# Seven quarter products for eighteen feed-forward up chunks, and the first modulation beside the cross attention

## The reference

```
def _conv_ffn(h, w_up, conv_w, conv_b, w_down):
    up = h @ w_up                       # 256x1024 @ 1024x5632
    up = conv over time, width 3, one filter a column, + conv_b
    gate, val = up[..., :D_FF], up[..., D_FF:]      # D_FF = 2816
    return (jax.nn.silu(gate) * val) @ w_down       # 2816x1024
```

## Time and profile before

| | |
|---|---|
| median of three runs | 1548.22 us |
| the profiled execution | 1547.08 us, its span 1545.3 us |
| granted TensorE clock, mean | 0.999 |
| TensorE matmul busy | 1498.7 us (97%) |
| TensorE weight load busy | 837.4 us (54%) |
| VectorE busy | 465.5 us (30%) |
| ScalarE busy | 320.1 us (21%) |
| DMA | 513.52 MB, mean 332 GB/s |
| chain that ended last | TensorE 80%, DMA 15%, VectorE 2%, ScalarE 1% |

### The profile page before, as it was taken

One profiled execution on the slowest core, in us unless ns is written; L12 is line 12 of the kernel. 1 busy time (PEld: TensorE's weight loads), 2 busy tenths in 40 slices (PEclk: granted clock), 3 DMA queues, 4 the chain that ended last, 5 costly groups with the idle time before them and its releaser, 6 DMA issues.

```text
span 1545.3 us, 18172 instructions
## 1 busy us (share of the span) xinstructions
PE 1498.7 (97%) x7042; PEld 837.4 (54%) x7042; DVE 465.5 (30%) x894; ACT 320.1 (21%) x660; POOL 22.3 (1%) x43
## 2 busy tenths in 40 slices
PE   9999999999999999899999899999989999999997
PEld 8667888888888755444333243433324433433432
DVE  3664125665642243522111121211211212121212
ACT  2443142111113353211011011101101101110112
POOL 0000000000000000000000000000000000000000
PEclk9999999999999999999999999999999999999999
DMA  9635444777751355899999999999999999999996
GB/s 379 282 111 197 156 166 165 272 268 267 270 202 55 109 217 194 347 405 428 428 428 428 428 425 422 428 430 428 428 428 427 411 426 429 426 427 427 428 427 273
DMA packets 46720, 513.52 MB, mean 332 GB/s; under 512 B 5264, under 2 KB 5408, under 8 KB 8384
## 3 DMA queue, kind: packets, MB, share of 16 engines
q1 hardware_dynamic: 41984, 482.53, 76.0%
q0 software_dynamic: 4672, 30.06, 5.2%
HBM read 511.51 MB, written 1.06 MB: 332 GB/s over the span
## 4 chain that ended last, share of the span: by engine, by line
PE 80%; DMA 15%; DVE 2%; ACT 1%; issue 1%; SPq 0%; DVEq 0%; ACTq 0%
PE bank L1369 31%; PE bank L745 13%; DMA ring<-in_gate_w 13%; PE bank L1005 9%; PE bank L1014 5%; PE bank L1333 3%; PE bank L1493 3%; PE bank L1401 3%; PE bank L1220 2%; PE bank L856 2%; DMA ring<-in_down_w 2%; PE bank L1386 2%; PE bank L1173 1%; PE bank L1162 1%; PE bank L1113 1%
## 5 line engine op out<-in xcount | busy, mean ns | idle before, releaser
L1369 PE MATMUL bank<-ring,probs_slab 128*64 128x512 f32 x2824 | 630.5, 596 | 25.5 <-DMA ring<-in_gate_w 14.5
L1369 PEld LDWEIGHTS bank<-ring,probs_slab 128*64 128x64 f32 x2824 | 194.8, 137 | 412.9 <-issue 373.9
L2588 DVE TENSOR_TENSOR squares<-bank,tab 128x512 f32<-128x512 f32 x31 | 21.4, 692 | 463.9 <-PE bank L1386 463.8
L1005 PE MATMUL bank<-normed,ring 128*128 128x256 f32 x672 | 146.9, 379 | 0.0
L1005 PEld LDWEIGHTS bank<-normed,ring 128*128 128x128 f32 x672 | 127.6, 190 | 18.0 <-issue 0.8
L745 PE MATMUL bank<-normed,ring 128*128 128x256 f32 x384 | 84.5, 381 | 0.4 <-ACT normed L1658 0.4
L745 PEld LDWEIGHTS bank<-normed,ring 128*128 128x128 f32 x384 | 72.2, 190 | 11.7 <-ACT normed L1658 1.2
L1014 PE MATMUL bank<-big_slab,ring 128*128 128x256 f32 x352 | 77.6, 379 | 0.0
L2596 DVE TENSOR_TENSOR squares<-bank,tab 128x512 f32<-128x512 f32 x31 | 21.4, 692 | 180.6 <-PE bank L1386 180.6
L1014 PEld LDWEIGHTS bank<-big_slab,ring 128*128 128x128 f32 x352 | 66.9, 190 | 9.1
L1979 ACT ACTIVATE squares<-bank 128x512 f32<-128x512 f32 x31 | 18.5, 597 | 227.2 <-PE bank L1369 227.2
(11 more groups left out here) (396 smaller groups left out, 1274.2 us busy)
## 6 DMA issues: line engine op xcount, KB each, us to landing
ring<-in_down_w SPq DMA_DIRECT2D x61, 2048.0 KB, 17.3
ring<-in_up_w SPq DMA_DIRECT2D x60, 2048.0 KB, 19.0
ring<-in_gate_w SPq DMA_DIRECT2D x58, 2048.0 KB, 18.9
ring<-in_front_w SPq DMA_DIRECT2D x72, 1024.0 KB, 5.0
held_slab<-in_mod_w POOLq DMA_DIRECT2D x6, 1024.0 KB, 8.6
memory_slab<-in_mod_w POOLq DMA_DIRECT2D x6, 1024.0 KB, 8.2
cross_keys_slab<-in_mod_w POOLq DMA_DIRECT2D x6, 1024.0 KB, 7.1
probs_turned_slab<-in_mod_w POOLq DMA_DIRECT2D x6, 1024.0 KB, 7.6
```

Source lines behind the costliest of these rows:

```text
L1005: mm = pe.matmul(bank[bank_at][:, half * T:(half + 1) * T], w[:, (half * DC + k) * P:(half * DC + k + 1) * P], H[:, k, :], start=(k == 0), ...
L1369: mm = pe.matmul(to[half * SLOTS:(half + 1) * SLOTS, :], tokens(k), weights[:, half * D + i * HALF:half * D + (i + 1) * HALF], start=(k == ...
```

## The change

For the 18 chunks 4 to 21 the up product is made of seven quarter products, Winograd's form of Strassen's scheme. The weights of a chunk are seen as two by two blocks (half of the input features; gate or value columns), the input `H` as two by two blocks (half of the features; half of the tokens). Each quarter product has four matmuls of 128x128 weights against 128 tokens. VectorE makes sums of the input blocks once (`ff_input_sums`), and for each chunk four differences of weight blocks of 512 columns, two iterations ahead (`ff_weight_sums`; one of them written in place in the ring). A chunk has two banks now, `own` and `shared`. ScalarE copies the first product and then three shared ones out between the matmuls (`read_first`, `read_shared`, `read_own`), TensorE goes on in the same columns of the banks, and VectorE puts the quarters together (`ff_merge`) in `ff_u`, from which base and taps read. A bank pair is free for chunk `f` when chunk `f - 2` is merged.

On ScalarE and VectorE the base and taps of a seven-product chunk come one iteration later, and ScalarE's silu of a chunk stands ahead of the copies of the chunk two behind it (for odd chunks behind the copy of the first product).

Round 0 of the modulation moves ahead: three chunks behind the first three output products `wo`, one behind the statistics of the input, one behind the first head sums, one behind the first query scale, two behind the last cross normalisation. Its sums and transposes on TensorE stand before up 0 and before the second pair. Rounds 1 and 2 go to the iterations in `MODULATED_AT`. POOL loads the weights by the new order, the DFT tables after the last up product, and the router's weights behind `co3`.

```
+SEVEN = list(range(4, FF_CHUNKS))
+MODULATED_AT = {1: [8], 2: [9], 3: [10], 7: [11, 12], 9: [13], 11: [14, 15], 13: [16, 17], 15: [18, 19], 17: [20, 21],
+                19: [22], 22: [23]}
...
@@ gpsimd
             full(pool, "vx11")
             load_mod(0)
             load_mod(1)
-            pool.wait_ge(s_cross_scored, XHEADS)
-            load_mod(2)
+            for n in range(2, DC):
+                pool.wait_ge(s_mod, mod_steps(n - 1))
+                load_mod(n)
             full(pool, "co3")
-            load_mod(3)
...
+            for n in range(DC, MOD_ROUNDS * DC):
+                pool.wait_ge(s_mod, mod_steps(max(n - 2, DC)))
+                load_mod(n)
+            pool.wait_ge(s_ff_up, FF_CHUNKS)
             pool.dma_start(DFT[:, 0:5, :], dft_in[:, 0:5, :]).then_inc(s_in["dft"], 16)
...
@@ tensor
+            def ff_bank_free(f):
+                if f - 2 in SEVEN:
+                    pe.wait_ge(s_ff_sums, MERGES[f - 2] + 4)
+                    pe.wait_ge(s_ff_read, 3 * SEVEN.index(f - 2) + 3)
+                else:
+                    pe.wait_ge(s_ff_conv, f - 1)
+
+            def ff_seven(f, w):
+                i = SEVEN.index(f)
+                own, shared = bank[2 * (f % 2)], bank[2 * (f % 2) + 1]
+                t1, t2, t4 = ff_b[i % 2]
+                s1, s2, s3, s4 = ff_a
+
+                def product(to, b, a, start=False):
+                    for k in range(4):
+                        mm = pe.matmul(to, b[:, k * P:(k + 1) * P], a[:, k, :], start=(start and k == 0), stop=True,
+                                       skip_group_check=True)
+                    return mm
+
+                product(own[:, 0:P], weight_part(w, 0, 0), token_half(0, 0), start=True).then_inc(s_ff_seven, 1)
+                pe.wait_ge(s_ff_sums, WEIGHT_SUMS[f] + 4)
+                product(shared[:, 0:P], t2, s2, start=True)
+                product(shared[:, P:2 * P], weight_part(w, 0, 1), s3)
+                product(shared[:, 2 * P:3 * P], t1, s1).then_inc(s_ff_seven, 1)
+                pe.wait_ge(s_ff_read, 3 * i + 1)
+                product(own[:, 0:P], weight_part(w, 1, 0), token_half(1, 0))
+                pe.wait_ge(s_ff_read, 3 * i + 2)
+                product(shared[:, 2 * P:3 * P], weight_part(w, 1, 1), s4)
+                product(shared[:, P:2 * P], t4, token_half(1, 1)).then_inc(s_ff_up, 1)
...
+            sum_modulation(0, bank[5]).then_inc(s_mod_sum, 1)
...
+            turn_modulation(0, bank[6]).then_inc(s_mod_turned, 1)
             ff_pair(1, first=True, early=True)
-            for s in range(2, 6):
-                ff_pair(s)
-            ff_pair(6, between=first_modulation)
-            pe.wait_ge(s_mod_taken, 1)
-            for s in range(7, 11):
+            for s in range(2, 11):
                 ff_pair(s)
...
@@ scalar (read_first copies own 128 columns, read_shared 384 shared ones, read_own 128 to ff_u)
+            for f in range(1, FF_CHUNKS):
+                if f % 2 and f in SEVEN:
+                    read_first(f)
+                if f - 2 in SEVEN:
+                    ff_silu(f - 2, (f - 2) % 4)
+                if f % 2 == 0 and f in SEVEN:
+                    read_first(f)
+                if f in SEVEN:
+                    read_shared(f)
+                if f - 1 in SEVEN:
+                    ff_base(f - 1, (f - 1) % 4, f - 1, f < 5)
...
+                if f in SEVEN:
+                    read_own(f)
...
@@ vector
-            add_products(["wo0", "wo1", "wo2", "wo3"], "xn")
+            dve.wait_ge(s_silu_c, 1)
+            add_products(["wo0", "wo1", "wo2", "wo3"], "xn", lambda j: modulate(0, j) if j < 3 else None)
...
+            def ff_weight_sums(f):
+                i = SEVEN.index(f)
+                w, slot, here = ff_ring(f)
+                t1, t2, t4 = ff_b[i % 2]
+                dve.wait_ge(chunk_here[slot], here)
+                if i >= 2:
+                    dve.wait_ge(s_ff_up, SEVEN[i - 2] + 1)
+                b00, b10, b01, b11 = [weight_part(w, k_half, half) for half in range(2) for k_half in range(2)]
+                dve.tensor_tensor(t1, b01, b00, SUB).then_inc(s_ff_sums, 1)
+                dve.wait_ge(s_ff_sums, WEIGHT_SUMS[f] + 1)
+                dve.tensor_tensor(b01, b11, b01, SUB).then_inc(s_ff_sums, 1)
+                dve.tensor_tensor(t2, b11, t1, SUB).then_inc(s_ff_sums, 1)
+                dve.wait_ge(s_ff_sums, WEIGHT_SUMS[f] + 3)
+                dve.tensor_tensor(t4, b10, t2, SUB).then_inc(s_ff_sums, 1)
+
+            def ff_merge(f):
+                i = SEVEN.index(f)
+                one, six, seventh, fifth = [ff_read[i % 2][:, j * P:(j + 1) * P] for j in range(4)]
+                dve.wait_ge(s_ff_read, 3 * i + 2)
+                dve.tensor_tensor(six, six, one, ADD).then_inc(s_ff_sums, 1)
...
+                dve.tensor_tensor(seventh, seventh, six, ADD).then_inc(s_ff_sums, 1)
...
+                dve.tensor_tensor(ff_u[i % 2][:, 3 * P:4 * P], fifth, seventh, ADD).then_inc(s_ff_sums, 1)
+                dve.wait_ge(s_ff_up, f + 1)
+                dve.tensor_tensor(ff_u[i % 2][:, P:3 * P].rearrange("p (c n) -> p c n", c=2),
+                                  bank[2 * (f % 2) + 1][:, P:3 * P].rearrange("p (c n) -> p c n", c=2),
+                                  over(six, 2), ADD).then_inc(s_ff_sums, 1)
...
             for f in range(1, FF_CHUNKS):
+                if f == FF_CHUNKS - 1:
+                    ff_merge(f)
+                    ff_taps(f - 1, (f - 1) % 4)
+                    ff_taps(f, f % 4)
+                else:
+                    if f - 1 in SEVEN:
+                        ff_taps(f - 1, (f - 1) % 4)
+                    if f in SEVEN:
+                        ff_merge(f)
+                    else:
+                        ff_taps(f, f % 4)
                 if f > 4:
                     dve.wait_ge(s_ff_down, (f - 1) // 2 - 1)
                 ff_gate(f - 1, (f - 1) % 4)
...
+                if f + 2 in SEVEN:
+                    ff_weight_sums(f + 2)
...
+                for n in MODULATED_AT.get(f, ()):
+                    modulate(n // DC, n % DC)
```

More of the change, by code:

```diff
@@ L115 @@
 FF_AFTER = len(STREAM)
+SEVEN = list(range(4, FF_CHUNKS))
+WEIGHT_SUMS, MERGES, _n = {}, {}, 4
+for _f in range(1, FF_CHUNKS):
+    if _f in SEVEN:
+        MERGES[_f] = _n
+        _n += 4
+    if _f + 2 in SEVEN:
+        WEIGHT_SUMS[_f + 2] = _n
+        _n += 4
+MODULATED_AT = {1: [8], 2: [9], 3: [10], 7: [11, 12], 9: [13], 11: [14, 15], 13: [16, 17], 15: [18, 19], 17: [20, 21],
+                19: [22], 22: [23]}
 STREAM += (
@@ L481, in build_program, with token_half, weight_part, ff_ring @@
         ff_act = [BIG[:, 8 + i, :] for i in range(4)]
+        wide = lambda s, i: s[:, i:i + 2, :].rearrange("p a n -> p (a n)")
+        ff_b = [[wide(HOLD, 0), wide(HOLD, 2), wide(HOLD, 4)], [wide(HOLD, 6), wide(SQ, 0), wide(SQ, 2)]]
+        ff_a = [wide(VX, 2 * i).rearrange("p (k t) -> p k t", k=4) for i in range(4)]
+        ff_u = [wide(SQ, 4), wide(SQ, 6)]
+        ff_read = [wide(BIG, 14), ff_second_read]
+        def token_half(k_half, t):
+            return H[:, 4 * k_half:4 * k_half + 4, t * P:(t + 1) * P]
+        def weight_part(w, k_half, half):
+            at = (half * DC + 4 * k_half) * P
+            return w[:, at:at + 4 * P]
+        def ff_ring(f):
+            q = f if f < 2 else 2 + 3 * (f // 2 - 1) + f % 2
+            c = FF_FIRST + q
+            return ring[:, (c % RING + FRONT_SLOT) % RING, :], c % RING, 16 * (c // RING + 1)
+        def ff_source(f, half):
+            if f == 0:
+                return first_up[:, half, :]
+            if f in SEVEN:
+                return ff_u[SEVEN.index(f) % 2][:, half * T:(half + 1) * T]
+            return bank[f % 4][:, half * T:(half + 1) * T]
         block = stack.enter_context(nc.Block())
@@ L1041, in _, with ff_pair @@
             ff_up_matmuls(1, ff_up(1, slot, here, True), lambda k: normed_chunk(pe, "f", k))
-            def ff_pair(s, first=False, early=False, between=None):
+            def ff_pair(s, first=False, early=False):
                 k = s
@@ L1048, in ff_pair @@
                     slot, here = ff_chunk(2 + 3 * (k - 1) + i)
-                    if between:
-                        between(i)
-                    ff_up_matmuls((2 * k + i) % 4, ff_up(2 * s + i, slot, here, early))
+                    f = 2 * s + i
+                    w = ff_up(f, slot, here, early)
+                    if f in SEVEN:
+                        ff_seven(f, w)
+                    else:
+                        ff_up_matmuls(f % 4, w)
                 slot, here = ff_chunk(2 + 3 * (k - 1) + 2)
@@ L2134, in modulate @@
                 n = r * DC + k
-                w = mod_w[n % 4]
-                dve.wait_ge(mod_here[n % 4], 16 * (n // 4 + 1))
+                w, i, count = mod_home(n)
+                dve.wait_ge(mod_here[i], 16 * count)
                 if k:
@@ L2327, in _ @@
             cross_normalise(3)
+            modulate(0, 6)
```

(14 more changed lines are left out.)

127 lines of the change are left out of this document (73 added, 54 removed).

## The result

The changed kernel took 1536.62 us (median of four runs, 1535.19 to 1538.33) against 1547.58 for the one before (median of four, 1546.72 to 1550.93). The ratio is 0.9926, with a 95% interval of 0.9907 to 0.9944: some 11 us faster, where 9.5 us and 1538.7 were predicted. The profiled execution, the fastest of the four, has a span of 1533.4 us for 1545.3 before, 11.9 us less.

The account below looks back on a forecast made before the run. TensorE was taken to bound the feed-forward. Terms: −11.4 (seven products) + 1.8 (waits) + 0.35 (modulation stall) − 0.2 (credit) = −9.5 us, from a median of 1548.2 to 1538.7 us; range 1533 to 1546.6.

Parts of the forecast that it names:

- TensorE bounds the stage, and time won in it reaches the end: Feed-forward: only TensorE in the chain from 241 to 473 us; the expert stream starts earlier by the gain, counted in full.
- The absorbed case: Rival, expert stage: its weight stream starts at the same time whatever TensorE does, 1548 us; chance 0.08.
- The cadence, 0.112 us a record: Seven-product up chunks: 56 records of 128 columns take 6.27 us against 6.91, 11.4 us won over 18 chunks.
- the full 7/8: Rival, up chunks: cadence 0.109 us and the copy never waited for, −14.4 us, 1533.8 us; chance 0.15.
- The rule of the Trainium skill: Up records: weight loads and matmuls together set spacing, 81 ns against 56 isolated; scaled, 0.158 us a record, 35 us lost.
- The rival of weight loads that bind: Up chunks: weight loads don't hide behind short records, cadence 0.13 us, 8.5 us lost, 1556.7 us; chance 0.09.
- The waits inside a chunk, 1.8 us: TensorE in seven-product chunks: 0.1 us a chunk for restarting behind the copy of three products; bounds 0 and 6.7 us.
- VectorE fits at 93%: Heaviest feed-forward pairs: VectorE needs 18.2 us of TensorE's 19.6 us a pair, at no cost.
- The rival in which it sets the pace: Heavy pairs: VectorE work 15% longer, pair 20.9 us, 6.5 us back, leaving 3.0 won, 1545.2 us; chance 0.10.
- The silu's new place, "nothing": ScalarE, odd chunks: silu behind the first product's copy, done 1.5 us into the chunk, inside the gate's 3 us; no cost.
- The modulation, +0.35 and −0.2: Moved modulation: VectorE work delays the first query product 0.35 us (bounds 0 and 0.8); 0.2 us credited in the feed-forward.
- The credit: Feed-forward: 0.2 us won because the up product behind the modulation's sums takes 7.11 us for 6.91.

Follow-up runs that it names:

- fifth product last: Changed kernel with the fifth quarter product of each seven-product chunk issued last, so the sixth stands right behind the fourth: 1552.30 us.
- silu behind the copy: Changed kernel with a chunk's silu behind ScalarE's copy of three shared products but ahead of the base of the chunk after: 1570.74 us.
- silu behind both: Changed kernel with a chunk's silu behind ScalarE's copy of three shared products and the base of the chunk after: 1597.89 us.
- the split alone: Kernel before the change with each up matmul of chunks 1 to 21 split by tokens into two of 128 columns, same arithmetic: 1553.74 us.
- The doubled copy: Changed kernel with ScalarE's copy of the three shared products done twice: 1544.50 us.
- three more additions a chunk: Changed kernel with three extra VectorE additions of 128x512, results unused, behind the weight sums of each seven-product chunk: 1548.12 us.

## Why the prediction was right, step by step

**TensorE bounds the stage, and time won in it reaches the end.** Right. 11.7 us are won by the end of the feed-forward and 11.9 at the end of the span; the first gather of the expert stage moved from 668.95 to 657.28 us, 11.7, and its stream behind it by as much. The other way round, the kernels whose product behind the feed-forward started 15.2, 32.7 and 60.6 us later (fifth product last; silu behind the copy; silu behind both) ended 16.4, 35.3 and 61.7 us later. The absorbed case is out.

**The cadence, 0.112 us a record.** Right, with 0.1116: 6.25 us a chunk, 0.655 won, 18 × 0.655 = 11.8 us for 11.4. The cadence of 0.109 that the full 7/8 needed is out by that, though its other half, a copy never waited for, came true. The gather's steady part was the row to take; the transposes' 0.109 and the whole gather's 0.115 were each off by the part that isn't a matmul of this form or isn't steady. The rule of the Trainium skill against this step ("TensorE: Matmul & The Clock Gate", Back-to-back issue gap), an estimate of 0.158 us by my scaling, isn't borne out: these f32 records run at 0.1116 in the changed kernel and in the split alone. The rival of weight loads that bind is out; they take 192 ns each, as in the gathers, and start 0.11 us apart, so two of them overlap.

**The waits inside a chunk, 1.8 us.** This is the term that was mis-sized: it is 0. The schedule (copy ends just before the fifth product does) was right to within 0.1 us, but I charged a restart that only a wait that is really met costs. The doubled copy shows that restart, 0.10 us, the size I had charged: there the sixth product's weight load and its first record start together at 304.35, behind the copy. In the changed kernel its load starts at 361.29, ahead of the record at 361.40 as everywhere else, so nothing was held back.

**VectorE fits at 93%.** Right, a little too high: 17.3 of 19.4 us with the small gaps, 89%, and no wait. The rival in which it sets the pace is real under load: three more additions a chunk cost 11.3 us, by the silu ahead of the copy, the path named in the prediction. Room for one (1.4 us a pair) is shown by the trace of the feed-forward alone.

**The silu's new place, "nothing".** Right as a cost, and far short as a part of the change: late, it costs 35 or 62 us. I had put its gate 3 us inside its time and not asked what the old order would have cost.

**The modulation, +0.35 and −0.2.** The stall of the first query product is 0.20 us (34.93 for 34.73). The credit didn't come: the product that follows the sums is still longer, 3.65 for 3.45, only now it is the first up chunk. Net 0.2 for 0.15. The last gate ends at 452.7 us, 1.5 before the last down product, for the 1.2 predicted.

In sum −11.8 + 0 + 0.2 = −11.6 us by the steps as measured, for −9.5 predicted.

## What to carry to other kernels

Where one engine fills a stage without a gap, a scheme that takes 1/8 of its arithmetic for more work elsewhere is worth what the shorter instructions' own cadence leaves of it; read that cadence from the steady part of the nearest stream of the same form, here within 0.4%. The rest of the work is then the queue order of the helping engines: what stands behind an instruction that may wait (weight sums behind a gate, a copy behind a silu) decides more than its own few tenths of a microsecond. An edit that moves nothing by itself can be what pays for another, so undo the parts one by one and also load the engine that was relieved.

## What the runs showed of the hardware that was not expected

After 4.40 us without a matmul TensorE's granted clock was 0.50 (1.2 GHz) for some 3 us from the restart and 1.00 after that: a down product of 7.07 us took 8.64. The seven waits of 3.35 to 4.77 us in that kernel were all followed by such a product, 1.6 to 1.8 us over. Shorter waits went either way: with the silu behind the copy alone the clock fell behind one of 2.55 us and not behind one of 3.15, and with three more additions it fell behind one of two waits of 1.92 us. So the price of a wait on TensorE can be near twice its length, and in these runs the length alone doesn't tell whether it is.

A wait on TensorE for a copy that ends as little as 0.21 us before the matmul behind it cost nothing that the trace shows: 56 records with three satisfied waits in between, one of them that close, run at 0.1116 us, the same as the 64 of a chunk in the split alone. When the wait is met, the product behind it takes 0.10 us longer than its records need.
